# Five stage boundaries of a two-block transformer kernel: the last panel, the norm and the first panels made for the first 256 tokens, then for the other 256

## What is computed

```
xl = xl + 0.5 * g1l * swiglu(modulate(rmsnorm(xl, norm_w[0]), sh1l, sc1l), w_ffn1_in, w_ffn1_out)
xc = xc + 0.5 * g1c * swiglu(modulate(rmsnorm(xc, norm_w[0]), sh1c, sc1c), w_ffn1_in, w_ffn1_out)
hl = modulate(rmsnorm(xl, norm_w[1]), sh2l, sc2l)
hc = modulate(rmsnorm(xc, norm_w[1]), sh2c, sc2c)
```

## Time and profile before

| | before |
|---|---|
| median of three runs | 4289.51 us (4289.47 to 4299.35) |
| the profiled execution's own time | 4287.59 us |
| its span in the trace | 4285.8 us |
| PE busy | 4187.1 us, 98% |
| DVE busy | 3071.4 us, 72% |
| ACT busy | 1793.0 us, 42% |
| mean granted TensorE clock | 0.993 |

### The profile page before, as it was taken

The page is one execution under the profiler, slowest core; times in us unless marked ns, Lnnn a source line. Parts: engine busy times, 40 slices in busy tenths (PEclk is TensorE's granted clock), DMA queues, the critical chain, the costliest instruction groups (busy, mean ns, idle before and its releaser), DMA issues.

```text
span 4285.8 us, 61414 instructions
## 1 busy us (share of the span) xinstructions
PE 4187.1 (98%) x24279; PEld 3729.0 (87%) x24279; DVE 3071.4 (72%) x4936; ACT 1793.0 (42%) x2976; POOL 1331.9 (31%) x699
## 2 busy tenths in 40 slices
PE   7999999999999999999999999999999999999999
PEld 5888778888888799867999999999999799998887
DVE  5775558877887686465599798788887675554776
ACT  3233352233233544263234786333334645444444
POOL 0000200000000100000378666777772058444443
PEclk9999999999999999999999999999999999999999
DMA  7543215544555364212477899999994166678884
GB/s 276 221 165 146 84 43 203 223 179 191 220 194 203 109 253 184 79 40 77 142 243 250 301 342 343 367 359 353 358 352 166 60 199 220 226 245 285 288 287 168
DMA packets 287199, 926.35 MB, mean 216 GB/s; under 512 B 19648, under 2 KB 171328, under 8 KB 212800
## 3 DMA queue, kind: packets, MB, share of 16 engines
q1 hardware_dynamic: 250048, 788.18, 51.8%
q0 software_dynamic: 36864, 134.23, 8.7%
HBM read 837.40 MB, written 84.93 MB: 215 GB/s over the span
## 4 chain that ended last, share of the span: by engine, by line
PE 86%; DVE 5%; DMA 4%; ACT 2%; POOL 1%; issue 1%; SPq 0%; ACTq 0%; POOLq 0%; DVEq 0%
PE bank L1132 25%; PE bank L1133 24%; PE bank L1134 24%; PE bank L1570 3%; DMA gates<-work 1%; PE bank L1325 1%; PE bank L1127 1%; PE bank L1122 1%; PE bank L1118 1%; PE bank L1337 1%; POOL weight_ring_low L2906 1%; PE bank L1362 1%; DVE work L2635 1%; DVE weight_ring_low L2246 1%; DMA work<-in_up_rows,work 1%
## 5 line engine op out<-in xcount | busy, mean ns | idle before, releaser
L2906 POOL TENSOR_TENSOR weight_ring_low<-weight_ring,up_high 128x1024 fp32r<-128x1024 f32 x233 | 586.4, 2521 | 1069.7 <-ACT up_high L1994 1067.6
L1134 PE MATMUL bank<-peer_h_high,weight_ring_low 128*128 128x256 f32 (+2 forms) x2240 | 698.3, 312 | 0.0
L1132 PE MATMUL bank<-peer_h_high,up_high 128*128 128x384 f32 (+1 forms) x2048 | 643.4, 314 | 14.3 <-POOL weight_ring_low L2906 7.4
L1133 PE MATMUL bank<-h_low,up_high 128*128 128x384 f32 (+1 forms) x2048 | 633.8, 309 | 0.0
L2081 ACT ACTIVATE down_high<-weight_ring 128x1024 fp32r<-128x1024 f32 x256 | 257.1, 1052 | 523.5 <-PE bank L1134 518.0
L1134 PE MATMUL bank<-h_high,weight_ring_low 128*128 128x512 f32 (+1 forms) x1280 | 463.9, 362 | 0.0
L1132 PE MATMUL bank<-h_high,in_high 128*128 128x512 f32 (+1 forms) x1216 | 441.1, 363 | 0.3
L1133 PE MATMUL bank<-h_low,in_high 128*128 128x512 f32 (+1 forms) x1216 | 440.8, 362 | 0.0
L2870 POOL TENSOR_SCALAR h<-work,params 128x256 f32<-128x256 f32 x12 | 11.8, 997 | 1376.7 <-PE bank L1477 874.6
L2662 DVE TENSOR_TENSOR weight_ring_low<-weight_ring,down_high 128x1024 fp32r<-128x1024 f32 x128 | 314.8, 2459 | 160.8 <-ACT down_high L2081 160.8
L1134 PEld LDWEIGHTS bank<-peer_h_high,weight_ring_low 128*128 128x128 f32 x2240 | 426.4, 190 | 3.7
(11 more groups left out here) (417 smaller groups left out, 10074.5 us busy)
## 6 DMA issues: line engine op xcount, KB each, us to landing
weight_ring<-in_up SPq DMA_DIRECT2D x128, 1024.0 KB, 6.0
weight_ring<-in_down SPq DMA_DIRECT2D x128, 1024.0 KB, 5.6
...
```

What stands on the lines that cost most here:

```text
L1132: mm(dst, w_high, a_high, start=first, stop=False)
L1133: mm(dst, w_high, a_low, start=False, stop=False)
L1134: return mm(dst, w_low, a_high, start=False, stop=last)
L2906: G.tensor_tensor(ring_low[:, slot, w], ring[:, slot, w], up_high[:, n % 3, :].bitcast(F32), ALU.subtract)\
```

## The change

At every norm that stands behind a feed-forward or mixer stage and has 512 tokens, and that is followed by another stage (five of them), the work is cut by tokens. The last output panel is made for the latents (all chunks), then for the context, into another bank (5). Between and within the context's half stand the sums of squares and the spreading of the latents' scales. The latents' columns of all eight chunks are then scaled, normed, rounded and split, and `halved_products` makes the four first panels for the latents (all high chunks, then all low ones, then the low weights), then for the context. The context's norm is written between. `keep_busy` is gone from these boundaries. Since the new stage's first two high weight units and its normed latents are now written while the old stage's last panel still reads its operands, they are put where operands that have been used up lie: for the feed-forward stages into the latents' columns, that is strided (`first_units`, `half_at`, `weight_view`). The buffers `out_high` and the waits of `round_out` and `split_out` are as they were, and so are `mod_sums` and its place. In the mixer before peer_0 the last panel's weights get a place of their own (`proj_last`).

```diff
+if s["joined"] and s.get("t") == T and "next" in s:
+    s["half"] = sum("half" in other for _, _, other in stages[:i])
+    s["late_bank"], s["late_scale"] = 5, 4
+    stages[i + 1][2]["halved"] = name, s
...
+first_units = dict(
+    ffn_ffn=((FC + 12) * T, 0), ffn_mix=(0, 18 * T), mix_ffn=(shared_at, shared_at + UNIT), even_peer=(shared_at, shared_at + UNIT))
+half_at = dict(ffn_ffn=8 * T, ffn_mix=(FC + 12) * T)
...
 def first_products(name, s, blocks):
+    if "halved" in s:
+        halved_products(name, s, blocks)
+        return
     r0, n0 = at[name]["rounds"], at[name]["normed"] - KC
...
+def halved_products(name, s, blocks):
+    r0, n0 = at[name]["rounds"], at[name]["normed"] - KC
+    norm, ns = s["halved"]
+    high, units, m0 = high_of(name)[0], halves[name][0], ns["half"] * KC
+    unit_block = lambda k, j: units[k][:, j // 2, j % 2 * P:j % 2 * P + P]
+    w = lambda j: slice(j * P, j * P + P)
+    pe.wait_ge(in_rounded, units_rounded(name, 0))
+    pe.wait_ge(second_rounded, at[name]["normed"] // KC)
+    for kc in range(KC):
+        pe.wait_ge(half_rounded, m0 + kc + 1)
+        for bank, k, j0, cols in blocks:
+            mm(ps[bank][:, LAT], unit_block(k, j0 + kc), high[:, kc, LAT], start=kc == 0, stop=False)
+        if kc == 3:
+            pe.wait_ge(squares_ready, at[norm]["square"] + KC)
+            column_sums(ns, norm, (2, 3), False, True).then_inc(summed, 1)
+    for kc in range(KC):
+        pe.wait_ge(half_split, m0 + kc + 1)
+        for bank, k, j0, cols in blocks:
+            mm(ps[bank][:, LAT], unit_block(k, j0 + kc), h_low[:, kc, LAT], start=False, stop=False)
+        if kc == 1:
+            pe.wait_ge(inverse_ready, at[norm]["norm"] + 1)
+            spread_scales(ns["late_scale"], (2, 3)).then_inc(panel_done, 1)
+    low_block = lambda k, j: ring_low[:, weight_unit(name, s, k) % SLOTS, w(j)]
+    for bank, k, j0, cols in blocks:
+        pe.wait_ge(in_split, r0 + k + 1)
+        for kc in range(KC):
+            i = mm(ps[bank][:, LAT], low_block(k, j0 + kc), high[:, kc, LAT], start=False, stop=kc == KC - 1)
+        if cols == TL:
+            i.then_inc(panel_done, 1)
+    blocks = [b for b in blocks if b[3] == T]
+    for kc in range(KC + 1):
+        if kc < KC:
+            pe.wait_ge(h_rounded, n0 + kc + 1)
+            for bank, k, j0, cols in blocks:
+                mm(ps[bank][:, CTX], unit_block(k, j0 + kc), high[:, kc, CTX], start=kc == 0, stop=False)
+        if kc:
+            pe.wait_ge(h_split, n0 + kc)
+            for bank, k, j0, cols in blocks:
+                mm(ps[bank][:, CTX], unit_block(k, j0 + kc - 1), h_low[:, kc - 1, CTX], start=False, stop=False)
+    for bank, k, j0, cols in blocks:
+        for kc in range(KC):
+            i = mm(ps[bank][:, CTX], low_block(k, j0 + kc), high[:, kc, CTX], start=False, stop=kc == KC - 1)
+        i.then_inc(panel_done, 1)
...
+def halved_panel(before, early_bank, terms, part, first_half=None):
+    norm, ns = before
+    last = len(terms) - 1
+    for n, term in enumerate(terms):
+        o = split_product(ps[early_bank][:, LAT], *part(term, LAT), n == 0, n == last)
+    o.then_inc(half_done, 1)
+    pe.wait_ge(squares_added, at[norm]["joined"] + KC - 2)
+    column_sums(ns, norm, range(4), True, False).then_inc(summed, 1)
+    for n, term in enumerate(terms):
+        o = split_product(ps[ns["late_bank"]][:, CTX], *part(term, CTX), n == 0, n == last)
+        if n == first_half:
+            o.then_inc(out_half, 1)
+        if n == (len(terms) + 3) // 4:
+            pe.wait_ge(half_squared, ns["half"] + 1)
+            column_sums(ns, norm, (0, 1), False, True).then_inc(half_summed, 1)
+        if n == len(terms) // 2:
+            pe.wait_ge(half_inverted, ns["half"] + 1)
+            spread_scales(ns["scale_bank"], (0, 1)).then_inc(half_spread, 1)
+    o.then_inc(panel_done, 1)
...
+if dc == KC - 1 and "half" in norm_of[name][1]:
+    def last_part(kc, cols):
+        half = kc // FH
+        w = slice((kc - half * FH) * P, (kc - half * FH) * P + P)
+        v = 2 * dc + half
+        return out_part(v)[:, w], ring_low[:, plan.out_unit[name][v] % SLOTS, w], ffn_high(kc)[:, cols], ffn_low[:, kc, cols]
+    for half in range(2):
+        pe.wait_ge(out_split, 2 * o0 + 2 * dc + half + 1)
+    halved_panel(norm_of[name], dc % 4, first_chunks + second_chunks, last_part, len(first_chunks) - 1)
+    continue
...
+def halved_norm(name, s):
+    high, half_h, n = high_of(s["next"][0])[0], halves[s["next"][0]][1], s["half"]
+    def normalise(src, dst, kc, half, done, ready, count):
+        A(src, src, ACT.Identity, bias=s["shift"][:, kc, half:half + 1], scale=s["gain"][:, kc, half:half + 1]).then_inc(done, 1)
+        act.wait_ge(done, count)
+        A(dst, src, ACT.Copy).then_inc(ready, 1)
+    def root(tiles, done):
+        A(square_sum[:, tiles], ps[s["sum_bank"]][:, tiles], ACT.Sqrt, bias=eps[:, 0:1], scale=1.0 / D).then_inc(done, 1)
+    act.wait_ge(half_added, n + 1)
+    act.wait_ge(summed, at[name]["summed"] + 1)
+    total, kc = squares_of(name, s, KC - 1), s["order"][KC - 1]
+    A(total[:, LAT], x[:, kc, LAT], ACT.Square).then_inc(half_squared, 1)
+    round_unit(*s["next"], 0)
+    act.wait_ge(half_summed, n + 1)
+    root(slice(0, 2), half_rooted)
+    for kc in range(KC):
+        act.wait_ge(half_scaled, n * KC + kc + 1)
+        normalise(half_h[:, kc, :], high[:, kc, LAT], kc, 0, half_normed, half_rounded, n * KC + kc + 1)
+        if kc == 3:
+            act.wait_ge(x_added, at[name]["added"])
+            A(total[:, CTX], x[:, s["order"][KC - 1], CTX], ACT.Square).then_inc(squares_ready, 1)
+        if kc == 5:
+            act.wait_ge(summed, at[name]["summed"] + 2)
+            root(slice(2, 4), root_ready)
+    for kc in range(KC):
+        act.wait_ge(scaled_ready, at[name]["scaled"] + kc + 1)
+        normalise(h[:, kc, CTX], high[:, kc, CTX], kc, 1, normed, h_rounded, at[name]["normed"] + kc + 1)
+    round_unit(*s["next"], 2)
...
+def halved_end(before, early_bank, gate, last_panel):
+    norm, ns = before
+    kc, n, half_h = KC - 1, ns["half"], halves[ns["next"][0]][1]
+    def add(bank, cols, half):
+        return V.scalar_tensor_tensor(x[:, kc, cols], ps[bank][:, cols], gate[:, kc, half:half + 1], x[:, kc, cols], ALU.mult, ALU.add)
+    dve.wait_ge(half_done, n + 1)
+    add(early_bank, LAT, 0).then_inc(half_added, 1)
+    round_second(*ns["next"])
+    dve.wait_ge(half_rooted, n + 1)
+    V.reciprocal(norm_scale[:, 0:2], square_sum[:, 0:2]).then_inc(half_inverted, 1)
+    dve.wait_ge(half_spread, n + 1)
+    dve.wait_ge(half_added, n + 1)
+    for k in range(KC):
+        V.tensor_tensor(half_h[:, k, :], x[:, k, LAT], ps[ns["scale_bank"]][:, LAT], ALU.mult).then_inc(half_scaled, 1)
+    dve.wait_ge(panel_done, last_panel)
+    add(ns["late_bank"], CTX, 1).then_inc(x_added, 1)
+def halved_norm(name, s):
+    to, n = s["next"][0], s["half"]
+    high, half_h = high_of(to)[0], halves[to][1]
+    def half_low(kc):
+        dve.wait_ge(half_rounded, n * KC + kc + 1)
+        V.tensor_tensor(h_low[:, kc, LAT], half_h[:, kc, :], high[:, kc, LAT].bitcast(F32), ALU.subtract).then_inc(half_split, 1)
+    def low(kc):
+        dve.wait_ge(h_rounded, at[to]["normed"] - KC + kc + 1)
+        V.tensor_tensor(h_low[:, kc, CTX], h[:, kc, CTX], high[:, kc, CTX].bitcast(F32), ALU.subtract).then_inc(h_split, 1)
+    for kc in range(5):
+        half_low(kc)
+    dve.wait_ge(root_ready, at[name]["root"] + 1)
+    V.reciprocal(norm_scale[:, 2:4], square_sum[:, 2:4]).then_inc(inverse_ready, 1)
+    for kc in range(5, KC):
+        half_low(kc)
+    dve.wait_ge(panel_done, plan.panel0[name] + 1)
+    for kc in range(KC):
+        V.tensor_tensor(h[:, kc, CTX], x[:, kc, CTX], ps[s["late_scale"]][:, CTX], ALU.mult).then_inc(scaled_ready, 1)
+        if kc == 1:
+            split_unit(*s["next"], 0)
+            split_unit(*s["next"], 1)
+        if kc >= 3:
+            low(kc - 3)
+    for kc in range(KC - 3, KC):
+        low(kc)
+    split_unit(*s["next"], 2)
```

67 lines of the change are left out of this document (59 added, 8 removed).

## The result

The changed kernel takes **4316.3 us**, median of ten runs (4309.0 to 4322.3); the kernel before, ten runs beside it, 4293.7 (4284.6 to 4301.7). The ratio is 1.0052, with a 95% interval from 1.0042 to 1.0063: slower by 22.6 us, 18 to 27 by the interval. The text above had 4303.0 us, range 4293 to 4315, and 13.5 us more than before. The direction was right, the size too small, and the range was missed by 1.3 us. Of the 13.3 us between 4303.0 and 4316.3, 4.2 are the median of before itself, which more runs moved from 4289.5 to 4293.7. Only executions in the usual, fast state enter the ratios of this text; one of e13's, further down, took 6897 us at a mean granted clock of 0.555 and is left out of its ratio.

What follows compares the result with a forecast made beforehand. PE, busy 98% of the span, was taken as the bound, with 8.5 us lost at most boundaries. Boundary costs of 11.7 us plus 1.75 for the clock made 13.5, put on the median 4289.51: 4303.0 us, range 4293 to 4315.

Steps and rivals of the forecast that it cites:

- Terms 1, 2 and 5: Boundaries: halved matmuls 9.1 us in all; sums and scales 2.6 a boundary; ACT's latents' chunks 0.95 apart, PE needing 0.48.
- Term 3: Ahead of the last feed-forward panel: PE waits 3.4 us for unit 15's split, at three boundaries.
- Term 4: Middle of the last feed-forward panel: PE waits for joined squares, 2.9 us at ffn2_0, 1.8 at ffn1_1.
- Term 6: Behind the idle stretch ahead of the last panel: clock at half rate 3.5 us, losing 1.75, counted at ffn1_0 only.
- Rival B: Around the boundaries: clock falls more often, at five more places that matter, 8.8 us more, 4312; chance 0.2.
- The third unit is split some 3 us before PE needs it: Start of the next stage: begins as before, costed at nothing; if that cover goes, 0.5 us at two boundaries.
- C: First high chunk and the panel's seam: operands ready, PE goes straight on, 19.7 us less, 4270; chance 0.1.
- D: ACT's latents' chunks: waits dearer on paper, chunks every 0.75 us would save 8 us, 4295; chance 0.2.

Runs made afterwards that it cites:

- e13: Changed kernel, all five boundaries: low blocks four chunks behind, unit splits in DVE's idle time, joined squares later, latents' root before first unit's rounding; ratio to before 1.0003.
- e1: Changed kernel plus seven keep_busy matmuls ahead of PE's wait for the last ffn panel's second weight unit; 4313.7 us, ratio to before 1.0048.
- e2: Changed kernel with the wait for the last ffn panel's second weight unit moved into the middle of the latents' half; 4308.8 us, ratio to before 1.0041.
- e12: Changed kernel with low blocks lagged, splits and joined squares moved, DVE reading 8 of 1024 columns of modulation units behind panel 6; 4288.4 us, 0.9989 to before.
- e8: Changed kernel with the third unit rounded behind the context's second chunk and split ahead of the last three low chunks; 4312.2 us, ratio to before 1.0043.
- e14: The kernel of e11 timed once more, nothing changed; 4287.0 us, ratio to before 0.9984.
- e6: Changed kernel with each latents' chunk's low matmuls right behind the next chunk's high ones, context's sums and scales later; 4327.3 us, ratio to before 1.0083.
- e11: Changed kernel at norm2_0, norm3_0, peer_norm_0 only: low blocks lagged, splits moved, latents' root before rounding, norm2_0's joined squares later; 4290.5 us, 0.9996 to before.

## Why the prediction was wrong

- **Terms 1, 2 and 5, and the mixer boundaries: right.** +1.13 and +1.10 for a foretold +1.1 each, latents' chunks 0.94 apart for 0.95.
- **Term 3: right.** 3.28 us for 3.4, at all three places, ended by DVE's split as said.
- **Term 4: right.** Joined squares waited for 2.62 us at norm1_1 for a foretold 2.9; at norm2_1 foretold 1.8 and 1.53 in e1, where the fall ahead of it is filled away (in the changed kernel that fall takes the wait's place, and no wait over 0.3 us is left). e2 and e12 show that it is DVE's queue behind `mod_sums`.
- **Term 6, the clock: the mechanism right, counted too rarely.** "It counts at ffn1_0; at ffn2_0 and ffn1_1 ... the joined squares are waited for anyway." I gave it one place, 1.75 us. It came at three that count: 1.5 us at norm2_0, 1.4 at norm1_1 and 1.6 behind norm2_1. I had let the waits of terms 3 and 4 swallow each other's falls, and did not ask whether the wait of term 4 brings one of its own behind it. Rival B had that, "in ffn2_0 it idles a second time", and its 4312 is nearest to what was measured. But it counted five more places that matter where there were two, and gave as its other mechanism that PE runs half empty behind ACT's pace: in the changed kernel the granted clock was 1.00 through that stretch of norm3_0 (622 to 630). The falls came at full stops.
- **"The third unit is split some 3 us before PE needs it": the step that failed.** It holds at norm2_0 (split by 430.2, needed at 433.56) and at the mixers, where PE spends 11.5 us on the context's 96 matmuls. At norm2_1 there are 48, the ACT chain has the same length, and the copy that frees mix_1's bank is queued behind the split. It cost 1.8 us, and the fall behind it; e8 took back both.
- Together: 1.4 and 1.8 and 1.6 us unforetold, 4.8, less 0.4 at norm2_0: 18.0 for 13.5, within a rounding. These steps alone would have left the forecast within its range, at 4307.5. With the 4.2 us by which the median of before moved it is 4311.7, still within; the last 4.6 are what stays open.
- **What stays open:** 22.6 were measured, 18.0 is in the boundaries; the interval just holds it. Over the runs e1 to e14 without e6, whose boundaries were 29 us longer and its time 36, measured loss and summed boundaries differ by -2 to +6 us, +1.9 in the mean. The traces say where it is not: the two stretches between norm3_0, norm1_1 and norm2_1 are 322.4 to 322.5 us long in all fourteen. In the profiled pair the stretch behind peer_norm_0 is 11.3 us longer (2286.8 against 2275.5), with up to 5.5 us in one wait for DVE's low weights where before has up to 4.0. But e11 and e14, one and the same kernel, have 2269.0 and 2279.4 there. So that stretch scatters by more than is sought, and whether any of the 4.6 belongs to the change is not shown.
- **Rivals C and D** fell: D with the chunks 0.94 us apart, C for the reasons given (the chunk's 0.95 us, the late split). But that the change must lose does not hold in general: with the stop moved, the splits and the root in other places, three of the boundaries are 1.4 to 2.9 us shorter than before.
